# Statistics of the first norm from the token rows, the neighbour table built after the first mixer, a reordered second mixer, a last store from ScalarE, and half of a query rotation on GpSimd

## The chip, the cores and the metric

One NeuronCore of one Trainium2 chip runs the whole program in one launch. The metric is the device time of one execution in microseconds (us), as the median of several runs.

## The reference: what is computed

Three layers of a transformer on one sequence of 256 tokens with 1024 channels, in float32. Layers 0 and 1 are feed-forward (FFN), mixer, FFN; the third is mixer, FFN. The mixer of layer 0 (the "even" one) joins a global attention of 8 heads, whose queries and keys are normalised per head and rotated, and a windowed attention of 8 heads with a sink, rotated only. The mixer of layer 1 (the "odd" one) is a neighbourhood attention of 16 heads with a table of relative biases (the "neighbour table"). The third mixer (the "second" one of the change's title) joins differential, windowed and latent attention. Cut to what matters here:

```python
for layer in range(2):
    x = x + 0.5 * swiglu(rms_norm(x, ffn1_norm[layer]), ffn1_w_gate[layer], ffn1_w_up[layer], ffn1_w_down[layer])
    h = rms_norm(x, mix_norm[layer])
    x = x + (even_mixer(h, ...) if layer == 0 else odd_mixer(h, ..., c_rel_bias, ...))
    x = x + 0.5 * swiglu(rms_norm(x, ffn2_norm[layer]), ffn2_w_gate[layer], ffn2_w_up[layer], ffn2_w_down[layer])
# rms_norm: x * rsqrt(mean(x*x) + 1e-6) * gain; D_FF = 2816
# rotation of a query head: q * cos + swap(q) * sin
# then the third layer (meta tokens, mixer "second", FFN) and a last rms_norm
```

## The kernel before, in words

Every weight matrix is cut into blocks of 128 x 1024 numbers (512 KB), 405 in all, which pass through a ring of six slots. For block n, SyncE issues the load (`load`, L518) once the low part of block n-6 is made; ScalarE copies it to a rounded high part (`split_hi`, L900); VectorE subtracts for the low part (`split_lo`, L1344); TensorE multiplies with high and low parts in float32r, three products for each pair of operands. Each engine has its order written out by hand, so a late load holds up all that stands behind its split on ScalarE and VectorE. An FFN has 22 tiles of the hidden width: a gate and an up block (`gate_up`, L2004), the gating (L1477 to L1498 on VectorE, L964 to L984 on ScalarE), and a down block (`cols_block`, L2016).

Opening. The token rows lie in `x_rows`, TensorE transposes them (L1937), VectorE copies them to `x` (L1368), ScalarE multiplies with the gain (L917) and VectorE makes the low part (L1385). After the first tile (`opening_tile`, L1981 and L1985) the norm's statistics are made: ScalarE squares `x` in four pieces (L925), VectorE adds them (`add_squares`, L1415 to L1420), TensorE sums over the partitions (`column_sums`, L1953), VectorE makes the mean (`mean_of`, L1432), GpSimd takes the power -0.5 (L640), TensorE spreads it to a row (L2124), which the gating needs.

GpSimd then issues 24 loads of constants (`load_constants`, L793 to L811), makes rotation tables (`axial_tables`), and builds the neighbour table (`near_table`): seven gathers from the biases to DRAM (L773, 256 KB each), then in two rounds a load of two times 448 KB (L781), the addition of a mask (L785) and a store (L788), through memory that is also the attention's bias buffer, and then the load of the query tables into the same memory (L790). The table is read first by the odd mixer.

Even mixer. For each of eight query chunks c, ScalarE copies the projection out of PSUM (`raw`, L1231), VectorE multiplies with the cosine table (`query`, L1587, counted by the semaphore `q_half`), TensorE swaps halves (`swap_query`, L2514), VectorE multiplies with the sine table and adds (`turn_query`, L1598 and L1602). GpSimd stores the distance biases and expands them to a table in DRAM (`expand_biases`, L759 and L764), then rotates the keys (`axial_keys`, L729 to L738) and makes the scales of the queries' heads (`query_scales`, L744 to L754).

Third mixer. Ten pairs of units j; for each, TensorE makes the scores of pair j+1, turns the probabilities of pair j (`second_turn`, L2287) and later multiplies with the values (`second_values`, L2321). Between these, 13 steps of the latent attention (`latent`, L2349 to L2369), which two PSUM banks take in turn. ScalarE and VectorE each copy one of two turned units out of PSUM (L1055, `copy_second_probs` L1671). VectorE makes the sums of scores and biases (`scores`, L1755) and the divisions (`normalise`, L1768 to L1783).

Tail. The output is stored in three pieces; SyncE issues the last (L613) after ScalarE's last instruction (L959).

## Time and profile before

| | us |
|---|---|
| median of 3 runs | 1300.41 (1298.82 to 1302.27) |
| profiled execution, its time | 1304.67 |
| its span, first to last instruction | 1302.6 |
| TensorE busy with matmuls | 1276.8 (98%) |
| VectorE busy | 996.7 (77%) |
| ScalarE busy | 733.9 (56%) |
| GpSimd busy | 128.8 (10%) |
| mean granted TensorE clock | 0.995 |

TensorE is busy for nearly all of the span. So the table is read for what is missing from it: 25.8 us in which TensorE does no matmul, and the few stretches in which its granted clock is lower. Where a stall is read, the question is which engine or transfer came last.

### The profile page before, as it was taken

To read this page: it belongs to the slowest core of one execution; us is meant where nothing else is said; L and a number is where in the kernel's file an instruction comes from. 1 tells how busy PE (TensorE), PEld (TensorE's weight loads), DVE (VectorE), ACT (ScalarE), POOL (GpSimd) and SP (SyncE) were. 2 spreads that over 40 slices of the span, in tenths; PEclk is the share of its full clock that TensorE was granted. 3 is DMA by queue.
4 is the path that set the end of the run, shared out by engine and by line. 5 is a ranking of instruction groups with operands and counts; after the bars stand their busy time and mean duration, and the time that the engine had idled before them with its cause. 6 is when DMAs were issued, how large, how long until landed. Compare 5 with 4: busy or idle time off the path is not lost.

```text
span 1302.6 us, 24400 instructions
## 1 busy us (share of the span) xinstructions
PE 1276.8 (98%) x8491; PEld 1139.2 (87%) x8491; DVE 996.7 (77%) x1864; ACT 733.9 (56%) x1327; POOL 128.8 (10%) x202
## 2 busy tenths in 40 slices
PE   7999999999999999999999999999999999999997
PEld 6989999789999998999989889999998968888886
DVE  6878778968877779777786769877776676877775
ACT  5545555766555556555565556555556554655553
POOL 3321002310000000000003202000005410000000
PEclk9999999999999999999999999999999999999999
DMA  9998655726766656666649537766657412666650
GB/s 262 267 248 267 188 186 149 174 78 197 211 185 186 192 162 197 191 192 187 185 144 260 178 102 233 214 186 192 190 156 175 141 46 81 198 191 189 183 175 33
DMA packets 295612, 233.57 MB, mean 179 GB/s; under 512 B 13180, under 2 KB 270532, under 8 KB 295552
## 3 DMA queue, kind: packets, MB, share of 16 engines
q1 hardware_dynamic: 288576, 214.07, 56.1%
q0 software_dynamic: 6688, 18.60, 5.8%
q8 instruction: 38, 0.62, 0.2%
q14 instruction: 22, 0.18, 0.1%
q10 hardware_dynamic: 288, 0.10, 0.0%
HBM read 229.79 MB, written 7.55 MB: 182 GB/s over the span
## 4 chain that ended last, share of the span: by engine, by line
PE 90%; DVE 4%; DMA 2%; ACT 2%; issue 1%; POOL 0%; POOLq 0%; ACTq 0%; DVEq 0%; SPq 0%
PE gu L2004 43%; PE y L2016 16%; PE y L2096 4%; PE gu L2385 4%; PE y L2058 3%; PE gu L2212 2%; PE y L2039 2%; PE gu L2181 2%; PE gu L2039 2%; DMA sb_w_raw<-in_ffn_w_gate 2%; PE gu L1971 1%; PE y L2423 1%; DVE sb_w_lo L1344 1%; PE gu L2400 1%; PE y L2412 1%
## 5 line engine op out<-in xcount | busy, mean ns | idle before, releaser
L2004 PE MATMUL gu<-sb_act_t,sb_w_hi 128*128 128x512 f32 x1680 | 589.2, 395 | 0.5 <-DVE sb_w_lo L1344 0.5
L1344 DVE TENSOR_TENSOR sb_w_lo<-sb_w_raw,sb_w_hi 128x1024 fp32r<-128x1024 f32 (+1 forms) x405 | 498.0, 1234 | 95.3 <-ACT sb_w_hi L900 89.3
L900 ACT ACTIVATE sb_w_hi<-sb_w_raw 128x1024 fp32r<-128x1024 f32 (+1 forms) x405 | 423.8, 1052 | 69.7 <-PE y L2016 30.9
L2004 PE MATMUL gu<-sb_act_t,sb_w_lo 128*128 128x256 f32 x1680 | 435.4, 280 | 0.0
L2004 PEld LDWEIGHTS gu<-sb_act_t,sb_w_hi 128*128 128x128 f32 x1680 | 308.1, 188 | 56.1 <-DVE sb_w_lo L1344 0.6
L2004 PEld LDWEIGHTS gu<-sb_act_t,sb_w_lo 128*128 128x128 f32 x1680 | 316.8, 189 | 14.9
L2016 PE MATMUL y<-sb_hid_t,sb_w_hi 128*128 128x256 f32 x1216 | 220.0, 281 | 3.1 <-DVE sb_hid_t L1498 3.1
L964 ACT ACTIVATE sb_work<-gu 128x256 f32<-128x256 f32 x220 | 83.7, 382 | 233.3 <-PE gu L2004 228.8
L2016 PEld LDWEIGHTS y<-sb_hid_t,sb_w_hi 128*128 128x128 f32 x1216 | 191.9, 189 | 6.8 <-DVE sb_w_lo L1344 3.4
L2016 PE MATMUL y<-sb_hid_t,sb_w_lo 128*128 128x256 f32 x608 | 170.9, 281 | 0.0
L1477 DVE TENSOR_TENSOR sb_work<-gu,sb_work 128x256 f32<-128x256 f32 x220 | 92.6, 423 | 95.9 <-ACT sb_work L964 95.8
L2016 PEld LDWEIGHTS y<-sb_hid_t,sb_w_lo 128*128 128x128 f32 x608 | 114.8, 189 | 0.0
L1481 DVE TENSOR_TENSOR sb_work<-sb_work 128x256 f32<-128x256 f32 x220 | 95.6, 436 | 7.6 <-ACT sb_work L984 0.4
L976 ACT ACTIVATE sb_hid_t<-sb_work 128x256 fp32r<-128x256 f32 x110 | 46.1, 419 | 83.4 <-DVE sb_work L1492 83.4
L640 POOL TENSOR_TENSOR sb_small<-sb_small 128x2 f32<-128x2 f32 (+3 forms) x16 | 19.4, 1212 | 554.2 <-DVE sb_small L1432 550.4
L969 ACT ACTIVATE sb_work<-sb_work 128x256 f32<-128x256 f32 x110 | 46.0, 418 | 28.1 <-DVE sb_work L1481 27.8
L1492 DVE SCALAR_TENSOR_TENSOR sb_work<-sb_work 128x256 f32<-128x256 f32 x110 | 46.8, 426 | 11.5 <-DVE sb_work L1481 0.5
L1041 ACT ACTIVATE sb_prob<-sb_prob,sb_small 128x256 f32<-128x256 f32 (+1 forms) x88 | 42.0, 481 | 15.0 <-DVE sb_small L1761 10.5
L1498 DVE TENSOR_TENSOR sb_hid_t<-sb_work,sb_hid_t 128x256 fp32r<-128x256 f32 x110 | 46.2, 420 | 5.3 <-ACT sb_hid_t L976 5.3
L1055 ACT ACTIVATE sb_prob_t<-y 128x512 f32<-128x512 f32 (+1 forms) x42 | 23.1, 586 | 47.7 <-PE y L2412 33.1
L1486 DVE SCALAR_TENSOR_TENSOR sb_work<-sb_work 128x256 f32<-128x256 f32 x110 | 46.1, 419 | 3.2 <-ACT sb_work L969 2.4
L2385 PE MATMUL gu<-sb_act_t,sb_w_hi 128*128 128x256 f32 x256 | 47.6, 287 | 0.0
(353 smaller groups left out, 1645.2 us busy)
## 6 DMA issues: line engine op xcount, KB each, us to landing
sb_w_raw<-in_ffn_w_gate SPq DMA_DIRECT2D x88, 512.0 KB, 3.9
sb_w_raw<-in_ffn_w_up SPq DMA_DIRECT2D x88, 512.0 KB, 3.9
sb_w_raw<-in_ffn_w_down SPq DMA_DIRECT2D x88, 512.0 KB, 3.8
sb_w_raw<-in_odd_w_qkv SPq DMA_DIRECT2D x24, 512.0 KB, 6.0
sb_w_raw<-in_w_gate SPq DMA_DIRECT2D x22, 512.0 KB, 3.9
sb_w_raw<-in_w_up SPq DMA_DIRECT2D x22, 512.0 KB, 3.9
sb_w_raw<-in_w_down SPq DMA_DIRECT2D x22, 512.0 KB, 3.6
sb_w_raw<-in_even_w_in SPq DMA_DIRECT2D x12, 512.0 KB, 3.8
```

The lines of the kernel that those rows point to most:

```text
L900: nc.scalar.activation(w_hi[:, slot, 0:w], w_raw[:, slot, 0:w], ACT.Copy).then_inc(hi_done, 1)
L964: nc.scalar.activation(halves[:, b, w, :], gu[:, b, w, SEQ:2 * SEQ], ACT.Copy).then_inc(half_copied, 1)
L1344: nc.vector.tensor_tensor(w_lo[:, slot, 0:w], w_raw[:, slot, 0:w], w_hi[:, slot, 0:w].bitcast(F32), ALU.subtract).then_inc(lo_done, 1)
L1477: nc.vector.tensor_tensor(sums[:, b, w, :], gu[:, b, w, 0:SEQ], halves[:, b, w, :], ALU.add).then_inc(gu_summed, 1)
L1481: nc.vector.tensor_tensor(sums[:, b, w, :], sums[:, b, w, :], rstd_row, ALU.mult).then_inc(scaled, 1)
L1492: nc.vector.scalar_tensor_tensor(out=hidden[:, b, :], in0=gated[:, b, :], scalar=0.5, in1=sums[:, b, 1, :], op0=ALU.mult, op1=ALU.mult).th ...
L1498: nc.vector.tensor_tensor(hid_t[:, h, 1, :], hidden[:, b, :], hid_t[:, h, 0, :].bitcast(F32), ALU.subtract).then_inc(hidden_split, 1)
L2004: ins = nc.tensor.matmul(gu[:, b, w, 0:width], part[:, s, cols], act_t[:, k, 0:width], start=(k == 0 and i == 0), stop=(k == KT - 1 and i ...
L2016: ins = nc.tensor.matmul(y[:, b, c * SEQ:(c + 1) * SEQ], part[:, s, cols], rhs, start=(first and c == 0 and i == 0), stop=False, skip_grou ...
L2039: ins = nc.tensor.matmul(mixed(kind, b)[:, c * SEQ:(c + 1) * SEQ], part[:, s, cols], rhs, start=(at == 0 and c == 0 and i == 0), stop=Fals ...
L2096: ins = nc.tensor.matmul(y[:, 2 * t + h, :], lhs[:, tok], part[:, s, h * 512:(h + 1) * 512], start=False, stop=False, skip_group_check=True)
L2385: ins = nc.tensor.matmul(gu[:, c % 2, 1, 0:SEQ], part[:, s, cols], rhs, start=(k == 0 and i == 0), stop=(k == KT - 1 and i == 2))
```

## The change

1. Opening: ScalarE squares the two tiles of token rows as they arrive (128x1024, with the sum along the row taken by the instruction), ahead of the first gains; GpSimd makes mean and power -0.5 from these sums. The four squares, four additions, the column sums and the mean go, for this norm alone. GpSimd's queue so starts its constants earlier.
2. The neighbour table is built after the first mixer (at the norm ahead of the second FFN) instead of in the first FFN; the query tables are loaded right after the constants.
3. Even mixer: the cosine half of the query rotation goes from VectorE to GpSimd (`half_query`), with two buffers; the gain or scale goes into the table ahead of it. The expansion of the distance biases moves behind the scales of the queries' heads.
4. Third mixer: the split of block 15 is moved from pair 3 to pair 4, behind the latent copies on ScalarE and the copy of probabilities on VectorE; the latent steps 8 and 12 come behind the scores of the next pair on TensorE; the high and low parts of the differential output come ahead of the exponentials and the divisions; for pairs 5 and 8 VectorE copies the probabilities between the two units' scores.
5. Tail: the last store is issued by ScalarE.

The diff, cut to its core:

```diff
@@ sync, end
-            sp.wait_ge(low_ready, 1)
-            sp.dma_start(out[0, P:2 * P, 0:512], xn[:, 1, 0:512]).then_inc(stored, 16)
-            sp.wait_ge(stored, 16 * 3)
+            sp.wait_ge(stored, 16 * 2)
+            sp.wait_ge(low_stored, 16)
@@ gpsimd, norm_rstd
+                if j == 0:
+                    pool.wait_ge(row_squares, TT)
+                    chain(nc.gpsimd.tensor_scalar(mean_sq[:, c:c + TT], sq_sum[:, c:c + TT], 1.0 / D, EPS, ALU.mult, ALU.add))
+                    power(rstd[:, c:c + TT], mean_sq[:, c:c + TT]).then_inc(rstd_ready, 1)
+                    return
@@ gpsimd, axial_keys
+                    if t == 0:
+                        half_query(2)
+            def half_query(c):
+
+                pool.wait_ge(table_scaled, 1)
+                pool.wait_ge(raw_copied, c + 1)
+                if c >= 2:
+                    pool.wait_ge(q_ready, c - 1)
+                nc.gpsimd.tensor_tensor(half_q(c), raw_q(c), q_tables[:, c // 4, 0, :], ALU.mult).then_inc(q_half, 1)
@@ gpsimd, query_scales
+                half_query(3)
+                half_query(4)
                 for pair in range(4):
...
+                    if pair < 3:
+                        half_query(pair + 5)
@@ gpsimd, near_table
-                pool.wait_ge(x_turned, 4)
-                pool.wait_ge(consts_loaded, 16 * N_CONSTS)
+                pool.wait_ge(x_updated, 4 * INDEX[2] + 4)
...
-                pool.wait_ge(near_stored, 64)
+
+            def query_tables():
+
+                pool.wait_ge(x_turned, 4)
+                pool.wait_ge(row_squares, TT)
                 pool.dma_start(q_turned, a["const"][:, N_CONST:N_CONST + N_TURNED]).then_inc(q_table_loaded, 16)
@@ gpsimd, order of the steps
                 if step == ("norm", 0):
                     load_constants()
                     axial_tables()
+                    query_tables()
+                    rows_rstd(meta_squares, 1, META, RSTD_COL[META_NORM], meta_rstd)
+                if step == ("norm", 2):
                     near_table()
-                    rows_rstd(meta_squares, 1, META, RSTD_COL[META_NORM], meta_rstd)
...
                 if step[0] == "mix" and step[2] == "even":
-                    expand_biases()
+                    store_distances()
+                    pool.wait_ge(q_table_loaded, 16)
+                    chain(nc.gpsimd.tensor_scalar(q_tables[:, 1, 0, :], q_tables[:, 1, 0, :], q_gain_col, None, ALU.mult))
+                    half_query(0)
+                    half_query(1)
                     head_norm(1, 16, 20, HD)
                     axial_keys()
                     query_scales()
+                    expand_biases()
@@ scalar, norm
                 if j == 0:
+                    c = RSTD_COL[0]
+                    for t in range(TT):
+                        act.wait_ge(x_loaded, 16 * TT)
+                        nc.scalar.activation(xn[:, t, :], x_rows[:, t, :], ACT.Square, accum_out=sq_sum[:, c + t:c + t + 1]).then_inc(row_squares, 1)
                     act.wait_ge(gain_ready, 1)
...
-                if j == 0:
-                    split_any(2)
-                    for b in range(4):
-                        nc.scalar.activation(x_sq[:, b, :], x_bank(b), ACT.Square).then_inc(squares, 1)
@@ scalar, final_norm
+                act.wait_ge(low_ready, 1)
+                act.dma_start(out[0, P:2 * P, 0:512], xn[:, 1, 0:512]).then_inc(low_stored, 16)
@@ scalar, second_mix
+                    if j == 4:
+                        split(15)
                     if pair[0].diff:
                         copy_probs(pair[1])
                     else:
                         copy_probs(pair[0])
+                    if j == 6:
+                        for i in range(2):
+                            act.wait_ge(diff_turned, i + 1)
+                            nc.scalar.activation(out_pair("second", 3 + i)[:, 0:SEQ], y[:, diff_bank(i), 0:SEQ], ACT.Copy).then_inc(diff_hi, 1)
...
-                    if j < 4:
+                    if j < 3:
                         split(9 + 2 * j)
@@ vector, even_groups (query and its calls go)
-                for s in range(2):
-                    ins = nc.vector.tensor_tensor(q_tables[:, 0, s, :], q_tables[:, 0, s, :], row6, ALU.mult)
-                chain(ins)
+                nc.vector.scalar_tensor_tensor(out=q_tables[:, 0, 0, :], in0=q_tables[:, 0, 0, :], scalar=HD ** -0.5, in1=row6,
+                                               op0=ALU.mult, op1=ALU.mult).then_inc(table_scaled, 1)
+                chain(nc.vector.tensor_tensor(q_tables[:, 0, 1, :], q_tables[:, 0, 1, :], row6, ALU.mult))
@@ vector, second_mix
-                        for un in SECOND_PAIRS[j + 1]:
-                            scores(un)
-                    copy_second_probs(j)
+                        scores(SECOND_PAIRS[j + 1][0])
+                        if j in COPY_BETWEEN:
+                            copy_second_probs(j)
+                        scores(SECOND_PAIRS[j + 1][1])
+                    if j not in COPY_BETWEEN:
+                        copy_second_probs(j)
+                    if j == 4:
+                        split(15)
+                    if j == 6:
+                        for i in range(2):
+                            diff_lo(i)
@@ vector and tensor, first norm
-                    add_squares(j)
+                    if j > 0:
+                        add_squares(j)
-                column_sums(j)
+                if j > 0:
+                    column_sums(j)
@@ tensor, second_mix
-                    for step in {4: (0, 1, 2), 5: (6, 7, 8), 6: (10, 11, 12)}.get(j, ()):
+                    for step in {4: (0, 1, 2), 5: (6, 7), 6: (10, 11)}.get(j, ()):
                         latent(step)
...
                     if j + 1 < len(SECOND_PAIRS):
                         second_scores(j + 1)
+                    for step in {5: (8,), 6: (12,)}.get(j, ()):
+                        latent(step)
```

## Rows read from the trace of the kernel before

**Rows 1.** TensorE's waits, whole span: engine line, what for, total us, times, longest.
```profile
PE gu L1931 <- DMA sb_gain_rows<-in_ffn_norm: 6.2, 1, 6.2
PE y L2016 <- DVE sb_hid_t L1498: 3.1, 1, 3.1
PE y L2321 <- DVE sb_prob_t L1671: 1.6, 2, 1.0
PE gu L2529 <- DVE sb_qt L1602: 1.2, 1, 1.2
PE gu L2247 <- ACT sb_work L1100: 0.9, 1, 0.9
PE y L2321 <- DVE sb_hid_t L1851: 0.6, 1, 0.6
PE gu L2364 <- DVE sb_qt L1662: 0.6, 1, 0.6
```

**Rows 2.** Busy time by stretch: engines' busy us, TensorE clock, DMA share, GB/s.
```profile
core 0: us, PE busy (x) PEld busy (x) DVE busy (x) ACT busy (x) POOL busy (x), PEclk, DMA share, GB/s
10.30:12.10 1.80, 0.70 (x2) 0.33 (x3) 1.60 (x4) 1.80 (x4) 0.00 (x0) 1.00 1.20 290
17.60:20.00 2.40, 0.68 (x6) 0.52 (x4) 2.33 (x5) 2.38 (x4) 0.00 (x0) 1.00 0.92 319
20.40:23.90 3.50, 3.50 (x13) 3.01 (x12) 3.46 (x8) 0.00 (x0) 1.07 (x2) 0.51 0.73 191
81.90:85.30 3.40, 3.40 (x18) 3.40 (x17) 3.33 (x7) 2.26 (x4) 0.62 (x2) 0.51 1.00 257
270.00:290.00 20.00, 20.00 (x166) 17.61 (x165) 11.41 (x31) 11.50 (x29) 1.71 (x4) 1.00 0.19 54
310.00:337.00 27.00, 27.00 (x180) 24.70 (x179) 23.71 (x40) 17.39 (x28) 0.00 (x0) 1.00 0.82 238
1047.80:1051.20 3.40, 3.40 (x17) 2.42 (x14) 2.37 (x11) 0.65 (x3) 0.00 (x0) 0.50 0.52 154
```

**Rows 3.** Timeline of the opening: start us, us, instruction, count, [idle before, releaser].
```profile
8.37 0.91 ACT L917 ACTIVATE sb_act_t<-sb_x,sb_gain_t 128x256 fp32r<-128x256 f32 x2 [2.25 <-DVE sb_x L1368]
14.01 2.35 DVE L1344 TENSOR_TENSOR sb_w_lo<-sb_w_raw,sb_w_hi 128x1024 fp32r<-128x1024 f32 x2
18.79 3.49 DVE L1344 TENSOR_TENSOR sb_w_lo<-sb_w_raw,sb_w_hi 128x1024 fp32r<-128x1024 f32 x3
23.25 1.22 DVE L1344 TENSOR_TENSOR sb_w_lo<-sb_w_raw,sb_w_hi 128x1024 fp32r<-128x1024 f32 x1
24.46 0.39 ACT L984 ACTIVATE sb_work<-y 128x256 f32<-128x256 f32 x1 [4.48 <-PE y L2124]
27.79 0.40 PE L2016 MATMUL y<-sb_hid_t,sb_w_hi 128*128 128x256 f32 x2
```

**Rows 4.** GpSimd's and ScalarE's timelines, 44 to 74 us: the gathers, a late gate block.
```profile
44.24 5.36 POOL L773 DMA_DIRECT2D near_dram<-in_c_rel_bias  x7
72.91 1.06 ACT L900 ACTIVATE sb_w_hi<-sb_w_raw 128x1024 fp32r<-128x1024 f32 x1 [5.36 <-DMA sb_w_raw<-in_ffn_w_gate]
```

**Rows 5.** DMA queues, 50 to 55 us: packets, MB, time as share of 16 engines.
```profile
q0 software_dynamic: 370, 1.21, 91.2%
q1 hardware_dynamic: 388, 0.21, 16.7%
```

**Rows 6.** Even mixer, VectorE's and GpSimd's timelines: one query half, one axial product.
```profile
232.01 0.42 DVE L1768 TENSOR_TENSOR sb_small<-sb_small 128x2 f32<-128x2 f32 x1
239.06 0.15 DVE L1768 TENSOR_TENSOR sb_small<-sb_small 128x2 f32<-128x2 f32 x1
240.90 0.42 DVE L1587 SCALAR_TENSOR_TENSOR sb_work<-sb_work,sb_bias_t 128x256 f32<-128x256 f32 x1
230.78 0.46 POOL L729 TENSOR_TENSOR sb_work<-sb_work,sb_axial 128x128 f32<-128x128 f32 x1 [0.17 <-POOL sb_small L670]
```

**Rows 7.** Tail, timeline: the issue of the last store.
```profile
1297.95 0.43 SPq L613 DMA_DIRECT2D out<-sb_work  x1
```

## What the change does to the time: the prediction

> **What bounds the kernel now.** I read the engines' busy table first: TensorE does matmuls for 1276.8 of 1302.6 us, so at most 25.8 us can be won without taking work from it, and the 6 us before the first weights and operands are there are no part of the change. Then I read TensorE's waits: the first in length behind the opening's 6.2 us is one of 3.1 us on a gating result, then several of 0.4 to 1.3 us in the even mixer and the third mixer [rows 1]. Then the busy time by stretch, for the clock: three stretches of 3.4 us stand at half clock (1.2 instead of 2.4 GHz), at 20.4, at 81.9 and at 1047.8 us, each right behind a stretch with idle TensorE [rows 2]. A stretch of 3.4 us at half clock does 1.7 us of work, so each costs 1.7 us on top of its gap. Together the waits that the change touches and these three stretches are about 15 us. All other work is a TensorE stream that the change leaves as it is. The profiled execution took 1304.67 us, 4.3 us more than the median of the runs; I come back to that below.
>
> **Opening.** Before, TensorE ends the first tile at about 17.6 us, then does 0.68 us of work in 2.4 us while it waits for VectorE's additions and for the low part of block 2 [rows 2, 3]; VectorE could have begun that low part at 16.36 us (14.01 + 2.35) but adds squares until 18.8. Without squares, additions and column sums, the three low parts (3.49 us) start 2.4 us earlier. ScalarE's added work is two 128x1024 squares. A 128x1024 activation with the copy function takes 1.05 us, as in the ScalarE row of a split (1.06) [rows 4]; with 0.2 us for reading the sum each, two take 2.3 to 2.5 us. ScalarE is free from 6.12 to 8.37 us (2.25 us ahead of the first gain) [rows 3], so they stick out by 0.1 to 0.4 us; I take 0.3, all of it on the path. Then: low parts 0 and 1 done at 16.7, 2 to 4 at 20.2, the gains and two additions by 21.3, the low part of block 5 (1.22 us) by 22.5. Before, that same low part ended at 24.47, and the row of the norm arrived at 24.85, 0.4 us later (24.46 + 0.39); from there it was 2.94 us to the first down product at 27.79 [rows 3]. After, the row is no longer last (GpSimd has it by 10 us, and TensorE spreads it within the tile by about 21), so 22.5 + 2.94 = 25.4: a gain of 2.4 us. TensorE meanwhile has finished its second tile. That is where the clock's part goes: if it stays high, the 16 steps of 0.36 us end at about 24.3, and TensorE waits 1 us for the gating; if it fell, they would end at 26. The idle is 1 us in place of 1.7, and the stretch with 1.1 us of idle at 10.3 to 12.1 kept its clock [rows 2], so I take the high one. Bounds: 1.5 us (a constant's load delays block 3 or 4) to 2.9 us (squares quite hidden). GpSimd's 24 constant loads move from 23 us to about 10 us, beside the first weights at a DMA share of 0.9 to 1.2 [rows 2]. The first tiles' loads are in flight already, and blocks 4 and 5 have 2 to 3 us before VectorE comes to them; that covers it, and it costs up to 1 us if not.
>
> **The neighbour table.** Its gathers and loads run from 44 to 73 us. While the gathers land, GpSimd's queue takes 91% of the engines' time and the weights' queue gets 0.21 MB in 5 us, of the 0.83 MB that TensorE uses up in that time (405 blocks of 0.524 MB in 1276.8 us) [rows 5]. At 72.91 ScalarE has waited 5.36 us for a gate block [rows 4]; VectorE stands behind it, the gating is late, and TensorE loses 3.1 us [rows 1] and then 1.7 us to the clock [rows 2]. So ScalarE may be late by some 2.2 us before TensorE feels it (5.36 less 3.1). Taken out of the first FFN this gives back 4.8 us. But the same transfers now start at about 309 us, in the second FFN, where the weights alone take 0.82 of the DMA time until 337 us [rows 2]. The Trainium skill, "DMA: Bandwidth & Descriptors", section on queues, rings and completion order, says that each DMA engine takes turns between queue rows packet by packet; by that rule large packets of GpSimd's queue crowd out the weights anywhere, and the trace agrees (91% against 17%) [rows 5]. What differs is the reserve. Before, the constants' loads had just run, at a DMA share near 1, when the gathers began; after, the six slots are full at 306 us. Carrying the weights' bytes of 50 to 73 us (0.21 MB, then about 0.2 MB a us) over to 314 to 337 us, I get ScalarE late by 2 to 2.7 us at its worst, against the 2.2 that cost nothing: 0.5 us. Net -4.3 us; bounds -4.8 (no stall) and 0 (the whole stall again). The load of the query tables moves from 108 us to about 32 us, when the ring is served; nothing.
>
> **Even mixer.** Eight products of 0.42 us (0.34 apart from the pipeline's overlap) leave VectorE [rows 6], 2.7 us in all, but TensorE is the bound and only its wait of 1.2 us for `q_ready` of chunk 4 [rows 1] hangs on VectorE; four or five products lie ahead of it, 1.4 to 1.7 us. Against it stands GpSimd's own load. A 128x128 product takes it 0.46 us [rows 6], so 128x256 takes about 0.85, and each of the eight is done 2 us or more before its `turn_query` (raw copies and turns stand one or two pairs apart). While GpSimd works on the keys, a VectorE operation of 0.15 us takes 0.42 [rows 6]: VectorE loses about a quarter of GpSimd's busy time, some 0.2 us for each half. That leaves 0.7 us, of which I take 0.6. Bounds: -1.2 and +1. The Trainium skill, "SBUF — State Buffer", section on who interferes with whom, says that GpSimd and VectorE exclude each other from a shared port for a whole instruction when VectorE has two inputs in SBUF; by it each half could hold VectorE for its full 0.85 us, 4 us for the first five, and the wait would grow. The row shows 0.27 us. Moving the expansion of the biases behind the scales puts its 5 us of issue and its transfers at 274 to 305 us, where the DMA engines are at a share of 0.19 at first [rows 2] (the odd mixer reads it some 370 us later); nothing, unless it runs into the weights of the second FFN, which I count to the case below.
>
> **Third mixer.** Four waits. (a) Latent step 2 waits 0.9 us on ScalarE's copy, which stands behind the split of block 15; the operands are there 0.4 us after the exponentials, so 0.4 is won, not 0.9. (b) Step 8 waits 0.6 for the rotation: the next scores (0.9 us) fill it. (c) The values of pair 5 wait 1.0 for VectorE's copy, which stood behind a unit's scores (0.85 us): 0.9. From (b) and (c) I take off 0.3, since step 11 now waits for a copy that follows the later exponentials. (d) The values of pair 6 wait 0.6 for the low part: gone; the exponentials behind it are 0.7 us later, under 6 us of other TensorE work. (e) Pair 8: 0.6 [rows 1] is given back at once, since the second unit's scores, exponentials and division are 0.7 us later and TensorE turns them next. Sum 0.4 + 0.6 + 0.9 - 0.3 + 0.6 = 2.2 us. The half clock at 1047.8 follows (a) at once; with 0.5 instead of 0.9 us of idle it may not come. It costs 1.3 us here (1.7 with dense work); I take half, 0.7. Bounds 1.0 to 4.
>
> **Tail.** The last store is issued at 1297.95, 0.25 us after the data is ready, since another issue stands ahead on SyncE [rows 7]: 0.2 us, bounds 0 and 0.4.
>
> **Sum**, against the profiled execution: 2.4 + 4.3 + 0.6 + 2.9 + 0.2 = 10.4 us, 1294.3. The runs' median lies 4.3 us below that execution, nearly the price of the table's stall, so some of the timed runs may not have it. I take 1 us off for that: 9.4 us from 1300.4 gives **1291.0 us**.
>
> **Rivals.** (A) The stall moves with the table: the ring at 310 us has to refill and uses 0.82 of the DMA time already, so one gate or up block is late by 5 us again. For it: the gathers crowd out any weights. Against it: full slots at the start. It gives 1291.0 + 4.3 = 1295.3 us. The same number comes if the timed runs never had the stall. (B) The halves on GpSimd hold VectorE up as the rule on the port has it: the wait of 1.2 us becomes 3: 1291.0 + 2.4 = 1293.4. (C) Slower: each of the three bursts (gathers, and the two rounds of 2 x 448 KB) stalls TensorE at 310 to 370 us like the one before, 3 x 4.8 = 14.4 us in place of the 0.5, while the timed runs had no such stall to lose: 1300.4 - 2.4 - 0.6 - 2.9 - 0.2 + 14.4 = 1308.7. It decides from the point at which ScalarE is over 2.2 us late for every burst; the second round before (85 to 97 us) stalled nothing, which speaks against it. (D) The opening gains nothing, since the gating chain is tied to late blocks 3 to 5 once the constants load beside them, and the table stalls again: 1291.0 + 2.4 + 4.3 = 1297.7.
>
> **How the numbers follow.** Forecast 0.58, A 0.20, B 0.08, C 0.04, D 0.05, and 0.05 for below 1286.5, where the clock stays high in the third mixer and the stall was in every timed run. The forecast's own range is 1286.5 to 1293.5. The range for 8 in 10 takes in A and B: 1286.5 to 1296.5. About 0.3% (3.9 us) is what a measurement of this kernel can tell from no change. Faster by more (under 1296.5): forecast, B, the low case and most of A, 0.86; within 0.3%: D and the rest of A, 0.10; slower: C, 0.04.
>
> **What would show it.** In the changed kernel: no half clock at 20 us and the first down product at 25.4; no wait of ScalarE on a weight load between 60 and 80 us; between 315 and 345 us such a wait of at most 3 us and a TensorE wait under 1 us; the wait for `q_ready` at the keys' turn under 0.8 us; TensorE's waits in the third mixer 1.5 us in all. The forecast is wrong if TensorE waits over 2 us in the second FFN, if ScalarE waits for blocks 3 or 4 in the opening, or if VectorE's operations beside the halves take twice their time.

## The result and the profile after

The changed kernel is slower. Its median is 1307.22 us (1305.72 to 1309.51) beside 1299.89 us (1298.82 to 1302.27) for the kernel before: a ratio of 1.0049, 95% interval 1.0028 to 1.0069. A second comparison, made later beside more executions of both, gave 1310.03 against 1302.13: 1.0077, interval 1.0051 to 1.0102. The loss is clear of both intervals and small, 0.5 to 0.8%. The forecast was 1291.0, with a range that ended at 1296.5.

The two profiled executions hide this: 1304.67 us before, 1305.72 after. The kernel before spreads over 1298.1 to 1306.5 us in its later executions, most of them between 1298 and 1301 or between 1302 and 1305.5, and the profiled one lay high; the changed kernel's profiled execution was the fastest of its first four. So I read from the traces where time went, stage by stage, and let the medians say how much.

The stages can be cut at one instruction, GpSimd's power for a norm's scale (line 640 before, 647 after). First the rows of before for the second, third and fourth norm, then those of after (timeline of GpSimd: start, duration, instruction, idle time before it and what ended that):

```profile
213.16 1.62 POOL L640 TENSOR_TENSOR sb_small<-sb_small 128x2 f32<-128x2 f32 x1 [23.30 <-DVE sb_small L1432]
307.03 1.61 POOL L640 TENSOR_TENSOR sb_small<-sb_small 128x2 f32<-128x2 f32 x1 [33.15 <-DVE sb_small L1432]
493.15 1.60 POOL L640 TENSOR_TENSOR sb_small<-sb_small 128x2 f32<-128x2 f32 x1 [184.51 <-DVE sb_small L1432]
```

```profile
207.40 1.61 POOL L647 TENSOR_TENSOR sb_small<-sb_small 128x2 f32<-128x2 f32 x1 [23.31 <-DVE sb_small L1475]
301.47 1.63 POOL L647 TENSOR_TENSOR sb_small<-sb_small 128x2 f32<-128x2 f32 x1 [28.72 <-DVE sb_small L1475]
497.19 1.62 POOL L647 TENSOR_TENSOR sb_small<-sb_small 128x2 f32<-128x2 f32 x1 [137.64 <-DVE sb_small L1475]
```

The first FFN gains 5.8 us (213.16 to 207.40), the even mixer changes by +0.2 (93.87 to 94.07), and the second FFN loses 9.6 (186.12 to 195.72). Further on, the same instruction shows +0.15 for the third FFN, +0.1 for the odd mixer, -3.2 from the norm behind it to the one behind the third mixer, and nothing for the rest. The sum is +1.1, which is what the profiled executions differ by.

TensorE's waits after the change, to be read beside [rows 1] (engine and line, for what, total us, times, longest):

```profile
PE y L2050 <- DVE sb_hid_t L1541: 7.6, 2, 6.1
PE gu L1965 <- DMA sb_gain_rows<-in_ffn_norm: 5.6, 1, 5.6
PE y L2050 <- issue: 1.5, 1, 1.5
PE gu L2564 <- DVE sb_qt L1635: 0.8, 1, 0.8
```

The wait on a gating result is still the longest that the change touches, and it grew from 3.1 to 7.6 us. The busy time by stretch (length, then each engine's busy us, TensorE's clock, DMA share, GB/s) says where, and what came behind it, as [rows 2] did for 81.9 us:

```profile
310.00:320.00 10.00, 10.00 (x67) 9.09 (x66) 6.74 (x12) 3.27 (x6) 0.67 (x2) 1.00 1.02 281
320.00:330.00 10.00, 8.52 (x57) 7.54 (x56) 6.20 (x10) 4.44 (x7) 0.61 (x2) 1.00 1.07 209
330.00:336.60 6.60, 4.36 (x26) 3.57 (x24) 3.68 (x1) 2.58 (x4) 4.16 (x2) 1.00 0.97 265
336.60:343.40 6.80, 2.90 (x13) 2.91 (x14) 6.63 (x11) 3.60 (x7) 1.13 (x2) 0.50 0.88 206
```

The DMA share is at 1 while TensorE starves, and then the granted clock is 0.50 for 6.8 us, not 3.4. TensorE has work for only 2.90 us of these, since its wait lasts until 340.50; so the half clock costs some 1.5 us here, by my estimate, and not more than the 1.7 of before. Who used the DMA engines is in the timelines of GpSimd and ScalarE:

```profile
267.67 5.08 POOL L793 DMA_DIRECT2D far_dram<-dist_dram  x3
303.07 5.37 POOL L801 DMA_DIRECT2D near_dram<-in_c_rel_bias  x7
319.33 1.28 POOL L809 DMA_DIRECT2D sb_bias_t<-near_dram  x2 [10.90 <-DMA near_dram<-in_c_rel_bias]
336.45 1.28 POOL L816 DMA_DIRECT2D near_dram<-sb_bias_t  x2 [0.30 <-POOL sb_bias_t L813]
320.12 1.06 ACT L939 ACTIVATE sb_w_hi<-sb_w_raw 128x1024 fp32r<-128x1024 f32 x1 [4.96 <-DMA sb_w_raw<-in_ffn_w_gate]
331.82 1.06 ACT L939 ACTIVATE sb_w_hi<-sb_w_raw 128x1024 fp32r<-128x1024 f32 x1 [5.25 <-DMA sb_w_raw<-in_ffn_w_gate]
```

Behind the gathers ScalarE waits 4.96 us for a gate block, at 320 us; TensorE feels 1.5 us of it. Before the ring recovers, the two loads of 448 KB issued at 319 us make ScalarE wait 5.25 us a second time, at 332 us, and TensorE waits 6.1. In the kernel before there was one such wait, 5.36 us at 72.91 [rows 4]; between its gathers and its loads the longest was 1.5 us:

```profile
60.65 1.06 ACT L900 ACTIVATE sb_w_hi<-sb_w_raw 128x1024 fp32r<-128x1024 f32 x1 [1.50 <-DMA sb_w_raw<-in_ffn_w_gate]
```

The late block is not all of the wait of 6.1 us, nor was it of the 3.1 before. Behind the two loads GpSimd adds the mask, an operation of 4 us, and a VectorE operation that runs beside it stands until it has ended. Here are the two operations before, and then after:

```profile
73.00 4.08 POOL L785 TENSOR_TENSOR sb_bias_t<-sb_bias_t,sb_const 128x1792 f32<-128x1792 f32 x1 [11.83 <-DMA sb_bias_t<-near_dram]
74.00 4.17 DVE L1344 TENSOR_TENSOR sb_w_lo<-sb_w_raw,sb_w_hi 128x1024 fp32r<-128x1024 f32 x1 [5.08 <-ACT sb_w_hi L900]
```

```profile
332.14 4.02 POOL L813 TENSOR_TENSOR sb_bias_t<-sb_bias_t,sb_const 128x1792 f32<-128x1792 f32 x1 [11.53 <-DMA sb_bias_t<-near_dram]
332.92 4.32 DVE L1387 TENSOR_TENSOR sb_w_lo<-sb_w_raw,sb_w_hi 128x1024 fp32r<-128x1024 f32 x1 [4.56 <-ACT sb_w_hi L939]
```

VectorE's subtraction takes 1.22 us elsewhere. So 2.95 of the 3.1 us before, and 3.1 of the 6.1 after, are VectorE held up by GpSimd's addition, and not by a DMA transfer. The addition moves with the table, and neither the prediction nor an experiment below takes it apart from the loads: its share is read from these rows.

A last line concerns the expansion that I had costed at nothing. SyncE's own queue, in the changed kernel:

```profile
287.61 8.95 SPq L526 DMA_DIRECT2D sb_w_raw<-in_ffn_w_up  x1
296.81 3.22 SPq L526 DMA_DIRECT2D sb_w_raw<-in_ffn_w_down  x1
```

Two issues of weight loads took 8.95 and 3.22 us, where such issues took 0.34 to 0.37 us in the kernel before in this stretch. The expansion's transfers had started at 267.67. A long issue alone need not cost time: before, one took 5.69 us at 66.98, beside the table's loads. What delayed the refill is that these blocks were late: ScalarE waits 1.56 us for one at 298.95, and the six slots are not full when the gathers start at 303.07.

### The profile page after: what moved, and what is told of

Its sections match the earlier page's. It is cut to its first block, busy times and chain, and to the rows that moved or that the text cites. A ratio compares the mean times of both kernels' runs of the same rounds, so it can differ in the third digit from the quotient of the medians.

```text
span 1303.8 us, 24389 instructions
## 1 busy us (share of the span) xinstructions
PE 1276.2 (98%) x8487; PEld 1137.7 (87%) x8487; DVE 996.5 (76%) x1851; ACT 734.7 (56%) x1327; POOL 135.4 (10%) x212
## 4 chain that ended last, share of the span: by engine, by line
PE 88%; DVE 4%; DMA 4%; ACT 2%; issue 1%; SPq 0%; POOL 0%; POOLq 0%; DVEq 0%; ACTq 0%
PE gu L2038 43%; PE y L2050 16%; PE y L2130 4%; PE gu L2420 4%; PE y L2092 2%; PE gu L2247 2%; DMA sb_w_raw<-in_ffn_w_up 2%; PE gu L2216 2%; PE y L2073 1%; DVE sb_w_lo L1387 1%; DMA sb_w_raw<-in_ffn_w_gate 1%; PE gu L2073 1%; PE gu L2275 1%; PE gu L2435 1%; PE gu L2504 1%
```

## The experiments

Three theories stood at first. Theory 1: expansion and table, both in the refilling of the ring for the second FFN, cost the time. Theory 2: the table's burst alone does. Theory 3 is the rival to both: other parts of the change cost it. Stage lengths of all runs stand in a table behind the last experiment.

**Table back in the first FFN.**

```diff
-                if step == ("norm", 2):
-                    near_table()
...
                     axial_tables()
+                    near_table()
                     query_tables()
```

> The changed kernel with the neighbour table built in the first FFN again, as before the change (the query tables are loaded behind it); the expansion of the biases stays late, behind the query scales. The changed kernel took 1307.2, the kernel before 1299.9. Theory 1 (GpSimd's two sets of transfers, expansion and then table, fall one after the other into the refilling of the ring for the second FFN, and together cost the 9.6 us that its trace loses between the norms at 301 and 497 us): the second FFN gets most of the 9.6 back, the first may stall again for up to 4.8: 1297.6 to 1302.4; TensorE waits under 1 us on gating results between 300 and 345 us. Theory 2 (the table's burst alone does it): the same range, and nothing at all is left of the wait. Theory 3 (the halves on GpSimd, the opening or the third mixer's order cost the time in the timed runs): 1303 or more.

1303.18 us, ratio 1.0010 (0.9995 to 1.0026). The second FFN is back at 186.14 us, and the first at 213.31. So the 9.6 us come only with the table in that place. In this one execution the stage of the even mixer is 1.5 us longer (95.62 us): ScalarE waits 3.1 us for a block at 306.46, and TensorE waits behind the norm. The FFN loses nothing. The saving of the rest of the change does not show in the median, though; that is taken up with the opening.

**Expansion back at the start of the even mixer.**

```diff
                     store_distances()
+                    expand_biases()
...
                     query_scales()
-                    expand_biases()
```

> The changed kernel with the expansion of the biases issued at the start of the even mixer, as before the change; the neighbour table stays in the second FFN. Theory 1 (it takes both): the six slots are full when the gathers start; TensorE's wait on the gating at 330 us falls from 6.1 to under 2 us and the half clock behind it goes: 1298 to 1301. Theory 2 (the table's burst alone does it): 1305 to 1308, and the wait stays at 4 us or more. Theory 3 (other parts): as theory 2 in time, but with no wait left at 330 us.

1306.30 us, ratio 1.0026 (1.0011 to 1.0041). The second FFN takes 193.04 us: 2.7 less than in the changed kernel and still 6.9 more than before. Waits of TensorE in this kernel:

```profile
PE y L2050 <- DVE sb_hid_t L1541: 4.5, 1, 4.5
PE gu L2435 <- DVE sb_qt L1635: 2.0, 1, 2.0
```

Theory 2 carries most of it, and theory 1 the rest: 6.9 us for the table alone, 2.7 for the expansion in front of it. In this trace the weights' ring has nothing left to load from 300 to 303 us (DMA share 0.00) and the gathers start at 304.66, so the six slots are full, and TensorE still waits 4.5 us. The second line is new. It also shows what the late place gains in the even mixer: issued early, the expansion holds GpSimd for 5 us ahead of the first halves, and the even mixer takes 95.50 instead of 94.07.

**Both back.** The two edits above together.

> Both sets of GpSimd's transfers back in their places of before (table in the first FFN, expansion at the start of the even mixer); left of the change are the opening, the halves on GpSimd, the third mixer's order and the tail. By the traces of before and after these are worth 1 (opening), 0 (halves), 3.2 (third mixer) and 0 (tail): theories 1 and 2 say 1299.9 - 4.2 = 1295.7, give or take 2. Theory 3 says 1300 or more.

1305.02 us, ratio 1.0012 (0.9996 to 1.0029), 9 us over what I expected, although its profiled execution (1302.70, the fourth fastest of twelve) adds up as the traces said: 211.94 + 96.45 + 186.13 and so on. Something in what is left (opening, halves, order, tail), or in the table beside the new opening, may cost time in the other executions, which have no trace. Theory 3 stays possible.

**Table paced in the second FFN, expansion early.** A gather for every third weight block, then each load and store behind a later block.

```diff
                 for r in range(n_rows):
+                    pool.wait_ge(lo_done, FIRST[3] + 14 + 3 * r + 1)
...
                     for i in range(2):
+                        pool.wait_ge(lo_done, FIRST[3] + 36 + 12 * g + 3 * i + 1)
                         pool.dma_start(halves_of[i], heads[i]).then_inc(near_loaded, 16)
...
                     for i in range(2):
+                        pool.wait_ge(lo_done, FIRST[3] + 42 + 12 * g + 3 * i + 1)
                         pool.dma_start(heads[i], halves_of[i]).then_inc(near_stored, 16)
```

> Expansion early as before, and the table in the second FFN but paced: a gather for every third weight block from the fourteenth on, then each load and store of its second half behind a later block (36, 39, 42, 45, and 12 later for the second group). If bursts into a ring that is refilling are the cause (theories 1 and 2), nothing stalls in either FFN: 1295 to 1298, and no TensorE wait over 1 us on a gating result. If the engines' share alone decides, wherever the transfers lie, it stalls in pieces: 1300 or more.

1299.89 us, ratio 0.9981 (0.9969 to 0.9993); the second FFN takes 186.12, with no wait on a gating result. The same bytes, at a lower rate and later (the first gather starts at 327.40 us), cost nothing. The spread is smaller too: 1298.1 to 1302.2, though in twelve executions only, where the kernel before has 1298.2 to 1306.5 in 35. Left is the wait behind the early expansion. The wait and its cause on GpSimd's timeline:

```profile
PE gu L2439 <- DVE sb_qt L1639: 2.8, 1, 2.8
217.51 4.81 POOL L793 DMA_DIRECT2D far_dram<-dist_dram  x3 [4.52 <-DMA dist_dram<-sb_kt]
223.40 1.40 POOL L761 TENSOR_TENSOR sb_work<-sb_work,sb_bias_t 128x256 f32<-128x256 f32 x2
```

**The same with the expansion late.** The changed kernel with only the table paced.

> The changed kernel with one edit: the neighbour table's transfers are paced in the second FFN (as in the paced kernel before), the expansion stays late, behind the query scales. The paced kernel with the early expansion profiled at 1298.5 with 96.25 us for the even mixer, where the late expansion has 94.07, and a wait of 2.8 us for the query operand of chunk 4. If the early expansion holds the halves up on GpSimd's queue: that wait is gone and the even mixer is back at about 94: 2.2 us less, profile 1296.3, timed median 1297 to 1299. If the late expansion alone stalls the refill of the ring at 300 us: TensorE waits in the second FFN for 1 us or more, and the two cancel: 1299 to 1301.

1299.02 us, ratio 0.9986 (0.9973 to 0.9998); the profile is at 1296.09, even mixer 94.10, second FFN 186.13. The wait of 2.8 us is gone, and the late expansion alone stalls nothing, although two weight-load issues take 8.04 and 3.20 us beside it here too. The 2.2 us of the even mixer are in the traces; the ratios of the two paced kernels, each beside its own executions of the kernel before, do not differ. This one edit turns the change from a loss of 0.5 to 0.8% into a gain of 0.1% (0.02 to 0.27).

**Expansion paced in the third FFN.** Each of its three transfers waits for a block there (15, 21, 27).

```diff
-                    expand_biases()
...
+                if step == ("norm", 3):
+                    expand_biases()
...
+                    pool.wait_ge(lo_done, FIRST[4] + {0: 15, P: 21, -META: 27}[key])
```

> As the paced kernel, but the expansion too is taken out of the even mixer and paced in the third FFN, one of its three transfers behind each of the blocks 15, 21 and 27: no transfer of GpSimd lies in any refill of the ring after the first FFN. Even mixer 93.9 to 94.1, second FFN 186.1, third FFN 190.6: profile 1296.3, median 1297 to 1299. If the late expansion costs nothing by itself, this is equal to the kernel with only the table paced; if it costs, this one is faster by 1 to 3.

1297.15 us, ratio 0.9966 (0.9953 to 0.9978), and only 2.7 us between the fastest and the slowest of ten. The stages differ from the kernel before this one by -0.3 (even mixer), +0.1 and +0.1; the profiled execution is not faster, so the 1.9 us in the median come from executions that no trace shows. Two things in the trace are not free. In the third FFN ScalarE now waits 5.1 us for a block behind the expansion's transfers, which the reserve takes up. And in the even mixer GpSimd's halves hold VectorE up: the first row below is VectorE's, beside a half (the second), and the third is the same operation in the kernel of a later experiment that has no half there:

```profile
242.38 1.12 DVE L1822 TENSOR_SCALAR sb_prob<-sb_prob,sb_small 128x256 f32<-128x256 f32 x2
242.36 0.73 POOL L761 TENSOR_TENSOR sb_work<-sb_work,sb_bias_t 128x256 f32<-128x256 f32 x1 [6.64 <-issue]
```

```profile
243.25 0.61 DVE L1814 TENSOR_SCALAR sb_prob<-sb_prob,sb_small 128x256 f32<-128x256 f32 x2
```

**Constants later.** On top of the last kernel, GpSimd's loads of the constants wait for the sixth weight block.

```diff
             def load_constants():
+                pool.wait_ge(loaded[5], 16)
```

> As the kernel with both paced, and the constants' loads wait until the sixth weight block has landed (about 19 us) instead of starting at 10 us beside it. In the traces with the new opening ScalarE waits 2.2 to 2.8 us for that block, and the first down product comes at 26.9 to 27.2 instead of the 25.4 predicted. If the constants beside the weights are why: the wait falls under 0.7 us, the first down product comes at 25.4 to 25.9, and the profile is 1.2 to 1.6 us under the kernel with both paced. If the first weights take that long anyway (the record of the clock is low until 15.8 us in these traces): 27, and no gain.

1297.68 us, ratio 0.9976 (0.9959 to 0.9994). The first down product comes at 24.97 us, a little under the 25.4 of my prediction. But the loads, now at 16.7 us, meet the next blocks, ScalarE waits 3.1 us there, and TensorE 1.5 us on the gating; the second tile's product is at 35.05, no better than 35.34 in the changed kernel.

**Constants after the 21st block.**

```diff
             def load_constants():
+                pool.wait_ge(lo_done, 21)
```

> As the kernel with both sets paced (1297.15), with the constants' loads held until VectorE has split the 21st weight block (about 55 us), where the ring has filled and the DMA share has fallen to 0.7. With the constants at 16.7 us the first down product came at 24.97 but the stall moved to the second tile (35.05, where it was 35.3 without). If the constants beside any early weights are the cause: first down product at 25.0, second tile at 33.4, third at 41.8, the first FFN ends 1.5 to 2.5 us earlier, profile 1293.5 to 1294.5, median 1295 to 1296, and a narrow spread. If ScalarE is late there by the weights alone: 1297 again.

1293.78 us, ratio 0.9951 (0.9933 to 0.9969): the best kernel, faster than both. First down product, then the same row in the changed kernel (timelines of TensorE):

```profile
24.62 0.47 PE L2058 MATMUL y<-sb_hid_t,sb_w_hi 128*128 128x256 f32 x2 [0.67 <-issue]
```

```profile
26.87 0.47 PE L2050 MATMUL y<-sb_hid_t,sb_w_hi 128*128 128x256 f32 x2 [1.48 <-issue]
```

In the changed kernel ScalarE waits for block 5, which lands beside the constants that GpSimd began to load at 9.73 us:

```profile
9.73 0.77 POOL L825 DMA_DIRECT2D sb_const<-in_const  x1
21.84 1.06 ACT L939 ACTIVATE sb_w_hi<-sb_w_raw 128x1024 fp32r<-128x1024 f32 x1 [2.19 <-DMA sb_w_raw<-in_ffn_w_gate]
```

In the best kernel ScalarE has no wait of that kind up to 110 us, the second tile is at 33.03 and the first FFN ends at 205.09, 2.3 us earlier than in the changed kernel and 3.7 earlier than in the kernel that differs by this edit alone (208.79). The 1.4 us between those two are a half clock in the opening that one execution has and the other has not: the first stretch below is of the changed kernel, the second of the kernel with both sets paced, with the same code up to there.

```profile
26.50:32.00 5.50, 5.13 (x37) 4.90 (x38) 4.95 (x8) 4.43 (x7) 3.50 (x5) 1.00 1.12 308
```

```profile
26.50:32.00 5.50, 5.24 (x29) 5.18 (x30) 4.94 (x7) 4.16 (x7) 3.57 (x6) 0.69 1.15 311
```

With the constants held back none of the traces has it. Repeated beside the last three experiments it gave 1294.15, ratio 0.9927 (0.9910 to 0.9943).

> The best kernel itself once more, as the base of these three: 1293.5 to 1296, 0.4 to 0.6% under the kernel before.

**The new opening alone,** on the kernel before, with table and expansion in their old places.

> The kernel before with the new opening alone; table and expansion in their old places. By the traces the opening gains 0.8 us at the second tile, and the kernel with table and expansion both back lost nothing in its profile, yet its timed median was 2.6 us over that of before. If the opening's earlier constants bring the table's gathers forward to where the ring is emptier: the stall in the first FFN is there in more of the runs, 1301 to 1305 as median, 0 to 3 us over before. If the opening is what it seems: 0.8 to 2.4 us under before. If the halves on GpSimd were the cause, this is under before too.

1306.04 us, ratio 1.0035 (1.0018 to 1.0052): alone, the opening makes the kernel slower. A likely reason is in GpSimd's timeline of this kernel:

```profile
31.05 5.37 POOL L780 DMA_DIRECT2D near_dram<-in_c_rel_bias  x7
45.79 1.27 POOL L788 DMA_DIRECT2D sb_bias_t<-near_dram  x2 [9.37 <-DMA near_dram<-in_c_rel_bias]
```

The norm's scale no longer holds GpSimd until 22.83, so the constants start at 9.4 and the gathers at 31.05 instead of 44.24 [rows 4], right behind the opening, where the ring has not caught up. The profiled execution was this kernel's fastest (1300.29), so no trace shows the slow ones, and that they are slow for this reason is argued and not shown. In this trace ScalarE waits 2.3 and 3.3 us for blocks behind the gathers and TensorE 0.5, and the first FFN (210.05) is still 3.1 us shorter than before. The kernel with the table back, which issues its gathers at 31.00 too, shows a wait of TensorE of 2.4 us behind them and a first FFN of 213.31. With the same opening and no table there, it is 207.40. So the table at 31 us costs 2.7 to 5.9 us in the three traces that have it there, about what it cost at 44. This is the part of theory 3, and it may be why neither kernel with the table put back was faster than the one before.

**The halves back on VectorE,** with everything else as in the kernel with both sets paced.

> As the kernel with both sets paced (1297.15, even mixer 93.8), but the cosine halves of the query rotation are back on VectorE, in its one buffer, as before the change. If the halves on GpSimd gain what I predicted (0.6 us): even mixer 94.4, and a wait of 1.2 us for the query operand of chunk 4. If they are worth nothing: within 0.3 of it. If they cost (the port): this is faster by 0.3 to 2.

1298.68 us against 1297.15, ratio 0.9977 (0.9962 to 0.9991) against 0.9966 (0.9953 to 0.9978): the intervals overlap. The even mixer takes 93.85 against 93.80 us. The wait for the operand of chunk 4 is 1.2 us again instead of 0.8, and as much is lost elsewhere: the halves on GpSimd are worth nothing in this stage. The 1.5 us between the medians are not in it; the profiled executions differ by 0.7 in the first FFN and 1.0 in the third. In the third TensorE waits 0.8 us on a gating here, beside the paced expansion; both kernels have that, and it does not come out the same in every execution.

**The third mixer's old order,** likewise.

> As the kernel with both sets paced, but the third mixer's order is that of before. By the profiles the order is worth 3.2 us (317.04 against 313.8 us from the sixth norm to the ninth). If that is real in the timed runs too: 1300.3, and the half clock at 1045 us is back; if the clock's part comes only in some executions: 1299 to 1300.3 with a wider spread.

1299.66 us against 1297.15: the order is worth 1.9 us in the stage (315.70 against 313.82). The medians differ by 2.5 us; by ratio, each beside its own executions of the kernel before, it is 0.9982 (0.9967 to 0.9996) against 0.9966, some 2.1 us, and the intervals overlap. The half clock at 1045 us was not back, which is the 1.3 us that the 3.2 of the first comparison had more.

**Which part of the burst, and which place.** Three kernels on the best one: the table unpaced but held until block 31 of the second FFN; the gathers at once at 300 us with loads and stores paced; and all of it at once at 300 us. The third edit, of which the others are halves:

```diff
-                    after_block(14 + 3 * r)
...
-                        after_block(36 + 12 * g + 3 * i)
...
-                        after_block(42 + 12 * g + 3 * i)
```

> The kernel that pays off best (constants late, expansion in the third FFN, table paced: 1293.8), with the pacing of the table taken away but its start held until the 31st weight block of the second FFN is split, near 385 us: the seven gathers at once, then loads and stores as they come. If a full ring is what counts (my blind argument, only its place was wrong): no TensorE wait, second FFN 186.1 to 186.3, 1293.8. If it is the burst itself, wherever it falls: TensorE waits 3 us or more, and 1297 to 1303.

> The same kernel, with the seven gathers issued at once at the start of the second FFN (300 us) and the loads and stores paced behind blocks 36 to 57 as they were. Splits the 6.9 us that the table's whole burst cost there. If the gathers make the stall: 4 to 7 us over 1293.8. If they only empty the ring and the loads behind them (2 x 448 KB at 319 us) tip it over: 0 to 1 us.

> The same kernel, with the whole table unpaced at 300 us, as in the changed kernel, but the expansion still in the third FFN and the constants late. If table and refill are the cause: the second FFN takes 193 us again (186.2 paced), TensorE waits 4 to 6 us near 333 us, 1299 to 1302. If the late expansion was needed for it: 1294 to 1296.

Held until block 31, so that it starts at 367.02 us: 1296.05 us, ratio 0.9935 (0.9919 to 0.9952), second FFN 186.12. The busy time of the stretch in which the unpaced gathers and loads run, in this kernel:

```profile
380.00:400.00 20.00, 20.00 (x139) 18.53 (x138) 15.06 (x21) 10.46 (x16) 5.36 (x4) 1.00 1.03 251
```

The DMA share is 1.03 as at 310 us in the changed kernel, and TensorE does not idle at all; ScalarE's waits for weights sum to 0.8 us. Gathers alone at 300 us: 1294.83, second FFN 186.85, and the waits of ScalarE and of TensorE there are

```profile
ACT sb_w_hi L946 <- DMA sb_w_raw<-in_ffn_w_gate: 3.9, 1, 3.9
PE y L2057 <- DVE sb_hid_t L1548: 0.5, 1, 0.5
```

All at once at 300 us: 1302.37 (1298.1 to 1305.4), second FFN 193.55, and

```profile
ACT sb_w_hi L944 <- DMA sb_w_raw<-in_ffn_w_gate: 7.8, 2, 4.0
PE y L2055 <- DVE sb_hid_t L1546: 5.3, 2, 4.7
```

So the same burst at the same rate costs 7.4 us in one place and nothing in the other. (A slow rate in the first place was not run: all paced kernels start their gathers at 322 us or later.) The gathers at once make one block 3.9 us late and cost 0.7 us; with the loads at 316 us and the addition behind them it is 7.4, with the expansion nowhere near. What is missing in the bad place is not the six slots of raw blocks. In the stretch ahead of the gathers, which start at 300.96, this kernel loads nothing, since the slots are full:

```profile
295.00:300.00 5.00, 5.00 (x31) 4.40 (x30) 4.82 (x9) 3.75 (x6) 0.60 (x1) 1.00 0.00 0
```

What is missing, as I read the rows, is the store behind them. A block that has landed is split by ScalarE and VectorE, and the split blocks have slots of their own. Behind the norm the kernel before splits a block every 2.35 us on average, from 306.73 us on, and the first wait of ScalarE for TensorE to free such a slot is at

```profile
332.58 1.06 ACT L900 ACTIVATE sb_w_hi<-sb_w_raw 128x1024 fp32r<-128x1024 f32 x1 [0.49 <-PE y L2016]
```

From there to 344.02 it is one per 2.86 us, and from 380 to 400 us the DMA share is 0.60. The burst at block 31 starts well behind that point, the two others ahead of it. The addition's part is in this kernel too: beside it a VectorE operation of 0.42 us takes 4.25, which is 3.8 of the 4.7 us that TensorE waits.

```profile
328.55 4.28 POOL L815 TENSOR_TENSOR sb_bias_t<-sb_bias_t,sb_const 128x1792 f32<-128x1792 f32 x1 [10.78 <-DMA sb_bias_t<-near_dram]
328.87 4.25 DVE L1534 SCALAR_TENSOR_TENSOR sb_work<-sb_work 128x256 f32<-128x256 f32 x1
```

In the kernel with the burst at block 31 a VectorE operation stands beside the addition as long (4.26 us at 396.52), and TensorE does not wait: there the reserve covers it. So a reserve that is not back, a late block and the addition come together; no run has the loads without the addition.

What the median of the burst at block 31 has over the best kernel's (1.9 us) lies in the third FFN and the third mixer of its profile (192.52 and 315.34 us). The third FFN holds the paced expansion, and there ScalarE waits 6.8 us for one block and TensorE 1.7 us on a gating. Over all kernels of the table below, that FFN takes 190.57 to 190.74 us without the expansion in it and 190.75 to 192.52 with it.

Stage lengths in us, from the starts of the power instruction; the last stage, 182.9, is the same in all. "n5 to n8" runs from the norm behind the odd mixer to the one behind the third mixer:

| kernel | FFN 1 | even | FFN 2 | FFN 3 | n5 to n8 | profiled | median |
|---|---|---|---|---|---|---|---|
| before | 213.16 | 93.87 | 186.12 | 190.58 | 317.04 | 1304.67 | 1299.9 to 1303.8 |
| changed | 207.40 | 94.07 | 195.72 | 190.73 | 313.80 | 1305.72 | 1307.22 |
| changed, second time | 207.69 | 94.09 | 195.41 | 190.62 | 315.30 | 1307.11 | 1310.03 |
| table back | 213.31 | 95.62 | 186.14 | 190.57 | 313.81 | 1303.27 | 1303.18 |
| expansion back | 207.59 | 95.50 | 193.04 | 190.74 | 315.25 | 1306.11 | 1306.30 |
| both back | 211.94 | 96.45 | 186.13 | 190.58 | 313.86 | 1302.70 | 1305.02 |
| table paced, exp. early | 207.62 | 96.25 | 186.12 | 190.66 | 313.87 | 1298.53 | 1299.89 |
| table paced | 207.34 | 94.10 | 186.13 | 190.67 | 313.85 | 1296.09 | 1299.02 |
| both paced | 208.79 | 93.80 | 186.19 | 190.81 | 313.82 | 1297.24 | 1297.15 |
| + constants at block 6 | 207.22 | 93.80 | 186.18 | 190.75 | 313.79 | 1295.56 | 1297.68 |
| + constants at block 21 | 205.09 | 93.79 | 186.17 | 191.08 | 313.82 | 1293.78 | 1293.78 |
| opening alone | 210.05 | 93.85 | 186.18 | 190.64 | 315.58 | 1300.29 | 1306.04 |
| halves on VectorE | 209.50 | 93.85 | 186.19 | 191.85 | 313.81 | 1299.02 | 1298.68 |
| old third order | 209.14 | 93.80 | 186.12 | 190.93 | 315.70 | 1299.51 | 1299.66 |
| burst at block 31 | 204.97 | 93.80 | 186.12 | 192.52 | 315.34 | 1296.57 | 1296.05 |
| gathers at once | 204.92 | 93.80 | 186.85 | 191.51 | 313.82 | 1294.72 | 1294.83 |
| all at once | 205.59 | 93.81 | 193.55 | 191.94 | 313.74 | 1302.45 | 1302.37 |

## Why the prediction was wrong, point by point

**The neighbour table: the step that failed.** The gain was as predicted: from the third tile's first down product (44.57 before, 43.73 after) to the end of the first FFN it took 168.59 us before and 163.67 after, 4.9 us against my 4.8. The new cost was 9.6 us against my 0.5. The step that failed is the one from "after, the six slots are full at 306 us" to ScalarE late by 2 to 2.7 us, of which 2.2 cost nothing, and so to 0.5 us. It was wrong in four ways.

- Full slots were no protection. Where they were full (expansion early, and all at once at 300 us), the table still cost 6.9 and 7.4 us. The 0.82 of DMA share that I quoted for 310 to 337 us [rows 2] was, by those rows, the store of split blocks filling behind the norm, not a steady state; with that store filled, as at block 31, the same burst cost nothing.
- In the changed kernel the slots were not even full, because of the expansion; see the next point.
- The 2.2 us that were to cost nothing (5.36 less 3.1) rested on a wrong reading. Of TensorE's 3.1 us, 2.95 were VectorE held up by GpSimd's addition. The late block alone would have been felt by some 0.2 us, and the addition, which moves with the table, had no term. After the change it is 3.1 of the 6.1 us.
- Before, the gathers had made ScalarE at most 1.5 us late and the loads 5.4; at 300 us both made it 5 us late. The gathers alone cost 0.7 us; the loads and the addition, 16 us behind them, met a reserve that the gathers had used up.

The range did not hold it either, as it ended at one stall of before's size. How the 7 us divide between loads and addition is read from rows, and stays open as an experiment.

**Where the 16.2 us between forecast and result lie.** The trace of the changed kernel is 11.4 us over the 1294.3 that the sum gave for it: 9.1 from the table and the expansion, 1.4 from the opening and the first FFN (5.8 gained, 7.2 in the sum), 0.8 from the even mixer, and small amounts elsewhere. The other 4.8 are in the step from the trace to the timed runs: I took them to lie 3.3 us under the profile, and they lay 1.5 above.

**The expansion of the biases: costed at nothing, worth 2.7 us** in the second FFN (195.72 against 193.04), together with the table; by itself nothing there (186.14 and 186.13), and 1.5 us in one execution at the norm. It makes the raw blocks late, so that their slots are not full when the gathers start. I had named the case "unless it runs into the weights of the second FFN" and then given it no term. Its transfers reach into the refill that starts at 286 us; the share of 0.19 that I read was that of 270 to 290 us alone.

**Rival C** was close in time, 1308.7 against 1307.22, and half right in mechanism. I had three bursts stalling TensorE at 4.8 us each, with a chance of 0.04. Two did (1.5 us behind the gathers, 6.1 us behind the first loads, then the half clock), 9.6 us together; the second round at 344 us stalled nothing, as I had held against it from the round before at 85 to 97 us. So the counter-argument was right, and too weak for 0.04: two bursts were enough. That the time came so close is partly luck, as the sum had 14.4 us of stalls where the trace shows 9.6. **Rival A** had the place and the size of ScalarE's wait right (4.96 and 5.25 us at a share near 1), and counted one where there were two.

**The opening.** The way was right, the place of the constants was not. I gave it 2.4 us with up to 1 us against it for the constants beside the first weights; the second tile's product gained 0.8 (36.17 to 35.34). With the constants out of the way the gain is 3.1 us (33.03), and the first down product is at 24.62, under the 25.4 worked out. So the constants cost 2.3 us, and 3.7 in executions with the half clock in the opening, not up to 1. The two squares on ScalarE were done at 8.52 us, 0.15 behind the 8.37 of before [rows 3], half of what I had taken. Not seen at all: that freeing GpSimd early also pulls its later transfers forward, from 44 us to 31 here. This part by itself is 0.35% slower in the medians; whether by this is argued, not shown. In the changed kernel the table had left, so this did not bite.

**The even mixer:** 0.6 us predicted, nothing measured. The wait for chunk 4 did fall from 1.2 to 0.8, but the stage did not shorten. Rival B (the halves hold VectorE up) came on VectorE and did not reach TensorE: an operation of 0.61 us took 1.12 beside a half, some 0.5 us where I had put 0.2, and the stage differs by 0.05 us between halves on GpSimd and halves on VectorE. The halves took 0.72 to 0.82 us each, under the 0.85 that I had estimated. The rule of the Trainium skill that I had weighed there ("SBUF — State Buffer", who interferes with whom) shows no price in this stage. The trace agrees with it at the table's addition, where I had not looked: 4.17 us instead of 1.22 for a VectorE subtraction of two inputs.

**The third mixer:** 2.9 us predicted, 3.2 in the first comparison, 1.9 in the stage and 2.1 to 2.5 in the medians when undone alone (with intervals that overlap). Right in mechanism and near in size; the clock's share (I took half of 1.3) comes and goes.

**The tail:** 0.2 predicted, nothing seen; the last issue comes 1.35 us behind the last power instruction instead of 1.51, but the span ends 6.31 us behind it after, 6.16 before.

**The base.** I took the price of the table's stall from one execution, saw that it lay 4.3 us over the median, and took off 1 us. Of the 95 later executions of the kernel before, 33 are under 1300.7 us, so there was less to gain in the median than in the profile. In numbers, the medians differ by 7.3 us where the traces differ by 1.1, because before's timed runs lie 4.8 us under its trace and the changed kernel's 1.5 over its own. What its slower executions do is in no trace.

## What to carry to other kernels

Before a background transfer is moved, ask of its new place how full the whole reserve is there, the split blocks as well as the raw ones, and not only how busy the DMA engines are: a share below 1 behind a norm can be a refill. Then count every burst of the set and the time between them: here the gathers alone cost 0.7 us, and with the loads and the addition behind them 7.4. Look also at what the issuing engine computes behind its transfers, since it moves with them. Tying each transfer to a block of the consumer's own progress took the table's cost in the second FFN to nothing (186.12 to 186.19 us); the expansion, tied in the same way in the third, still cost 0.2 to 1.9 us. An edit that frees an issuing engine early moves everything queued behind it forward, so look up what that is.

## What the runs showed of the hardware that I had not expected

**The same idle time does not bring the same clock.** In the changed kernel TensorE was busy for 3.45 of 4 us at 1047 us, in both profiled executions. In one the clock then stayed at 2.4 GHz, in the other it went to 1.2 GHz (busy time by stretch, first and then second execution):

```profile
1047.00:1051.00 4.00, 3.45 (x26) 2.85 (x24) 3.20 (x16) 3.62 (x14) 2.12 (x4) 1.00 0.78 234
1051.00:1056.00 5.00, 5.00 (x33) 4.16 (x32) 3.62 (x14) 4.11 (x15) 0.00 (x0) 1.00 0.00 2
```

```profile
1047.00:1051.00 4.00, 3.45 (x25) 2.86 (x24) 3.14 (x16) 3.62 (x14) 2.12 (x4) 0.97 0.83 236
1051.00:1056.00 5.00, 5.00 (x26) 3.82 (x25) 2.65 (x12) 2.59 (x7) 0.00 (x0) 0.68 0.00 1
```

That is 1.5 us in this stage (313.80 and 315.30) without any edit. A stall's second price, the clock, has to be given as a chance. The opening does the same: with the same code, its clock fell in some executions (0.69 from 26.5 to 32 us) and not in others (1.00). Behind the wait of 6.1 us the clock was low for 6.8 us, where each of the three stretches before was 3.4; but TensorE worked for 2.90 of these only, against 3.40 before, so the price was no higher.

**A transfer beside an issue.** Weight-load issues of some 0.35 us took up to 8.95 us on SyncE's queue while GpSimd's expansion was being moved, and up to 5.69 us in the kernel before beside the table's loads. An issuing queue that looks idle in the busy table can be stuck. It need not cost time: with the table paced and the expansion late, an issue took 8.04 us and the second FFN 186.13.

**VectorE stands still for a GpSimd operation.** In eight traces a VectorE operation that runs beside the mask's addition on GpSimd (4 to 5 us) ends about its own length behind the end of that: 4.17 us instead of 1.22 before, 4.25 instead of 0.42 with all at once at 300 us. Beside the halves it is 1.12 us instead of 0.61. Whether TensorE feels it depends on the reserve of split blocks: it lost 3.8 us by it in one place, and nothing in the other.
